# Hybrid decoder layer with 64 experts: the shared expert's down products in nine pieces, the first token lists among its gate and up tiles, the sorting in seven steps

## What is computed

```python
def _moe(x, p):
    scores = sigmoid(xf @ p['w_router'])              # 264 x 64
    ...                                               # group-limited top 8 of 64 experts
    gate = sum(one_hot(eidx, 64) * wsel[..., None])   # weight of each token for each expert
    def expert_block(xb, gb):
        h = silu(einsum('td,edf->tef', xb, w_gate)) * einsum('td,edf->tef', xb, w_up)
        h = h * gb[..., None]
        return einsum('tef,efd->td', h, w_down)       # w_gate, w_up: 1024x256, w_down: 256x1024 each
    routed = expert_block(...)
    shared = (silu(xf @ p['ws_gate']) * (xf @ p['ws_up'])) @ p['ws_down']
    return routed + shared

y = h + _moe(rmsnorm(h)); output = rmsnorm(y)
```

## Time and profile before

| what | us |
|---|---|
| median of 3 runs | 1104.72 |
| the three runs | 1104.01, 1104.72, 1107.85 |
| span of the profiled execution, first to last instruction | 1106.8 |
| TensorE busy | 967.0 (87%) |
| VectorE busy | 531.6 (48%) |
| GpSimd busy | 347.4 (31%) |
| ScalarE busy | 230.3 (21%) |

### The profile page before, as it was taken

The page is one execution under the profiler, slowest core; times in us unless marked ns, Lnnn a source line. Parts: engine busy times, 40 slices in busy tenths (PEclk is TensorE's granted clock), DMA queues, the critical chain, the costliest instruction groups (busy, mean ns, idle before and its releaser), DMA issues. The chain is left out here.

```text
span 1106.8 us, 17738 instructions
## 1 busy us (share of the span) xinstructions
PE 967.0 (87%) x7221; PEld 564.4 (51%) x7221; DVE 531.6 (48%) x1014; ACT 230.3 (21%) x476; POOL 347.4 (31%) x396
## 2 busy tenths in 40 slices
PE   5999999999999978788998798897987878789896
PEld 4878777877877775356333333333333323323231
DVE  2158759766875868745621111111112335424685
ACT  3241134115113411430211111111111111111012
POOL 0059609914970892001011101101013213312330
PEclk9999999999999998889999998988989888989999
DMA  8535244234524192395699999999999999999931
GB/s 236 188 118 183 97 131 168 108 125 131 189 85 154 45 330 73 155 359 187 239 394 418 418 417 412 412 404 405 401 403 400 401 375 379 401 415 402 387 98 41
DMA packets 98972, 295.65 MB, mean 267 GB/s; under 512 B 19603, under 2 KB 50901, under 8 KB 82232
## 3 DMA queue, kind: packets, MB, share of 16 engines
q1 hardware_dynamic: 80695, 254.02, 60.1%
q0 software_dynamic: 18192, 40.46, 9.8%
HBM read 284.12 MB, written 36.30 MB: 290 GB/s over the span
## 5 line engine op out<-in xcount | busy, mean ns | idle before, releaser
L1278 PE MATMUL bank<-big 64*64 64x64 f32 (+7 forms) x6778 | 910.9, 367 | 117.1 <-DMA big<-in_w_up 70.5
L1278 PEld LDWEIGHTS bank<-big 64*64 64x64 f32 (+3 forms) x6778 | 516.7, 152 | 462.1 <-issue 378.6
L1577 ACT ACTIVATE big<-bank 128x512 f32<-128x512 f32 (+6 forms) x283 | 121.2, 450 | 714.6 <-PE bank L1278 396.9
L1075 POOL DMA_INDIRECT big<-xg,big x32 | 32.3, 1008 | 404.2 <-PE bank L561 353.3
L919 DVE TENSOR_TENSOR big<-big,bank 128x256 f32<-128x256 f32 x32 | 13.4, 420 | 239.3 <-ACT big L1577 239.3
L2069 POOL TENSOR_SCALAR big<-big 128x256 f32<-128x256 f32 x120 | 124.5, 1038 | 1.7
L2081 POOL TENSOR_TENSOR big<-big 128x256 f32<-128x256 f32 x120 | 86.2, 718 | 0.3
L1867 DVE SCALAR_TENSOR_TENSOR big<-big 128x256 f32<-128x256 f32 x120 | 78.7, 656 | 4.1
L979 DVE SCALAR_TENSOR_TENSOR big<-big 128x1024 f32<-128x1024 f32 (+1 forms) x48 | 61.4, 1280 | 17.3 <-DMA big<-yrows,big 14.1
L1092 POOL DMA_INDIRECT big<-yrows,big x48 | 51.2, 1067 | 51.0 <-DVE big L979 28.4
L1577 ACT ACTIVATE big<-big 128x272 f32<-128x272 f32 (+8 forms) x104 | 48.2, 509 | 46.7 <-DVE big L814 12.3
(11 more groups left out here) (163 smaller groups left out, 406.5 us busy)
## 6 DMA issues: line engine op xcount, KB each, us to landing
big<-in_w_gate SPq DMA_DIRECT2D x64, 1024.0 KB, 15.8
big<-in_w_up SPq DMA_DIRECT2D x64, 1024.0 KB, 20.4
big<-in_w_down SPq DMA_DIRECT2D x64, 1024.0 KB
big<-in_w_in SPq DMA_DIRECT2D x29, 1024.0 KB, 5.3
yrows<-big POOLq DMA_DIRECT2D x32, 512.0 KB, 3.5
big<-in_w_out SPq DMA_DIRECT2D x2, 2048.0 KB, 16.2
big<-in_state_wkv SPq DMA_DIRECT2D x32, 64.0 KB, 2.2
out_wkv_s<-big SPq DMA_DIRECT2D x32, 64.0 KB, 3.8
```

The lines of the kernel that those rows point to most:

```text
L1075: pool.indirect_dma_start(out=x[0:n, :], out_offset=None, in_=xg, in_offset=bass.IndirectOffsetOnAxis(ap=idxu[0:n, col:col + 1], axis=0), ...
L1278: return nc.tensor.matmul(out_, lhsT=lhsT, rhs=rhs, start=start, stop=stop)
L1577: return nc.scalar.activation(out_, in_, f, **kw)
```

## The change

- The shared down matrix is no longer loaded first into slot 3; it is loaded after the gate and up of expert 3 into a place of its own, `wsd` (two of the five row buffers `early` that are first used in pair 19). SP no longer waits for `shd_mm`; the down matrix of expert 3 is loaded with the first loads.
- The down products are cut into nine pieces: four of 256 columns for each block of 128 rows (two matmuls each), and one for the sample rows (eight matmuls). TensorE does piece n at the start of iteration 4 + n, between `index` and the first half of `gate_up`. All use one half of bank 5, whose other half takes the turned hidden values; so `turn_hidden(q-1)` in that iteration also waits until the piece has been added (`shy_ready`).
- VectorE adds piece n in `pair(4 + n)`, ahead of `hidden`; for the sample rows ScalarE copies and VectorE adds in pair 12.
- The tiles `shared_gate_up(1, 0)` and `(1, 1)` are cut into halves, and the lists 0, 1 and 2 and `turn(0)` stand between the halves.
- The sorting becomes a generator, `rows_and_gates`, of which one step is done after each of `pair(1)` to `pair(7)`. The two buffers that hold `wsd` are no longer cleared; the third is cleared by VectorE in the last step and not by GpSimd ahead of pair 0.

A load that waited for the down products is replaced by one that waits for nothing of its own. The diff, cut:

```diff
@@ moe_sp
-            for part, n in enumerate(('ws_gate', 'ws_up', 'ws_down')):
+            for part, n in enumerate(('ws_gate', 'ws_up')):
                 load_item(sp, part, SHARED_SLOT, A[n][0])
...
+            load_item(sp, 2, 3, expert_w(2, 3))
...
-            sp.wait_ge(S['shd_mm'], 5)
-            load_item(sp, 2, 3, expert_w(2, 3))
+            sp.dma_start(wsd, A['ws_down'][0].rearrange("(j p) d -> p j d", p=128)).then_inc(S['wsd_in'], 16)
@@ moe_pe
+            def shared_down(n):
+                if n == 0:
+                    pe.wait_ge(S['wsd_in'], 16)
+                    pe.wait_ge(S['shh_ready'], 2)
+                wait(pe, 'shy_ready', n)
+                t, i = divmod(n, 4)
                 for j in range(2):
...
+                    if t < 2:
+                        ins = mm(ps_sd, hsh[:, j, 128 * t:128 * t + 128], wsd[:, j, QD * i:QD * i + QD], j == 0, j == 1)
+                    else:
+                        for i in range(4):
+                            ins = mm(ps_sd[32 * i:32 * i + NS, :], hsh[:, j, NP:NT], wsd[:, j, QD * i:QD * i + QD],
+                                     j == 0, j == 1)
                 note(ins, 'shd_mm')
...
@@ turn_hidden
+                if 0 < q + 2 - DOWN_AT < NDOWN:
+                    pe.wait_ge(S['shy_ready'], q + 2 - DOWN_AT)
+                elif q + 2 - DOWN_AT == NDOWN:
+                    pe.wait_ge(S['shs_ready'], 6)
...
-            for q in range(3):
-                index(q)
-            shared_gate_up(1, 1)
-            pe.wait_ge(S['shh_ready'], 2)
-            pe.wait_ge(S[f'wd_in{SHARED_SLOT}'], 16)
-            shared_down(0)
+            index(0)
+            shared_gate_up(1, 0, KT // 2, KT)
+            index(1)
+            shared_gate_up(1, 1, 0, KT // 2)
+            index(2)
             pe.wait_ge(S['cnt_ready'], 1)
             turn(0)
+            shared_gate_up(1, 1, KT // 2, KT)
...
-                if q == 0:
-                    pe.wait_ge(S['shy_ready'], 2)
+                if q == 1:
+                    pe.wait_ge(S['shh_ready'], 2)
+                if DOWN_AT <= q < DOWN_AT + NDOWN:
+                    shared_down(q - DOWN_AT)
                 gate_up(q, 0, 4)
-                if q == 0:
-                    shared_down(1)
-                    shared_down(2)
...
@@ moe_dve
+                if DOWN_AT <= q < DOWN_AT + NDOWN - 1:
+                    shared_rows(q - DOWN_AT)
                 hidden(q)
...
+            rows = rows_and_gates()
             for q in range(1, NPAIR):
                 pair(q)
+                next(rows, None)
@@ moe_pool
-            for x in early[2:]:
-                link(gp.memset(x, 0.0), 'xe_zero')
...
```

More of the change, by code:

```diff
@@ L755, in moe_act @@
             turned(0)
-            act.wait_ge(S['shd_mm'], 5)
-            for i in range(4):
-                note(fn(shs[0:NS, QD * i:QD * i + QD], ps_sd[4][32 * i:32 * i + NS, 0:QD], ACT.Copy), 'shs_ready')
             for q in range(NPAIR):
+                if q == DOWN_AT + NDOWN - 1:
+                    act.wait_ge(S['shd_mm'], NDOWN)
+                    for i in range(4):
+                        note(fn(shs[0:NS, QD * i:QD * i + QD], ps_sd[32 * i:32 * i + NS, :], ACT.Copy), 'shs_ready')
                 if q:
@@ L904, in shared_hidden, with shared_rows @@
                 note(v.tensor_tensor(hsh[:, j, :], sgs[:, j, :], ps_sh[2 + j][:, 0:NT], M), 'shh_ready')
-            def shared_rows(t):
-                for h in range(2):
-                    dve.wait_ge(S['shd_mm'], 2 * t + h + 1)
-                    x = xrow[:, t, 512 * h:512 * h + 512]
-                    note(v.tensor_tensor(x, x, ps_sd[2 * t + h][:, :], AD), 'shy_ready')
+            def shared_rows(n):
+                t, i = divmod(n, 4)
+                if t < 2:
+                    dve.wait_ge(S['shd_mm'], n + 1)
+                    x = xrow[:, t, QD * i:QD * i + QD]
+                    note(v.tensor_tensor(x, x, ps_sd, AD), 'shy_ready')
+                else:
+                    dve.wait_ge(S['shs_ready'], 6)
+                    note(v.tensor_tensor(xrow[0:NS, 2, :], xrow[0:NS, 2, :], shs[0:NS, :], AD), 'shy_ready')
             onehot(0)
```

113 lines of the change are left out of this document (59 added, 54 removed).

## The result

The changed kernel takes 1094.38 us (median of 4 runs, 1092.86 to 1096.27) beside 1105.84 us for the kernel before on the same chip (1104.01 to 1107.85): a ratio of 0.9892, with a 95% interval of 0.9869 to 0.9915. That is 11.5 us less. Two later comparisons of the same two kernels gave 0.9923 (0.9899 to 0.9947) and 0.9895 (0.9868 to 0.9922), so the gain is some 8.5 to 12 us. The profiled execution of the changed kernel took 1092.86 us around a span of 1091.1 us. In every run here 1.8 us lie around the span, so the profiled execution of the kernel before, with its span of 1106.8 us, took about 1108.6 us: it is none of the four, and some 2.8 us above their median. Its trace stands for a somewhat long execution.

The account below looks back on a forecast made before the run. The prediction took the weight stream to bound the expert loop, its unbroken start setting the end. 12.0 us up to pair 0 plus 0.5 from the sorting made 12.5, from 1104.72 to 1092.2 us, range 1088.5 to 1098.

Parts of the forecast that it names:

- The end follows the start of the stream, not TensorE's work: Expert loop: weights set the pace, so bringing SP's releases at 538.35 and 551.16 us forward brings all that follows forward.
- 12.0 us up to the end of pair 0: Token mask to pair 0's gate and up: 12.2 us removed, 0.2 us waiting at `turn(0)`, ending 12.0 us earlier at 526.2.
- parts for the down products: Before and inside pair 0: moving the shared down products away takes off 4.1 us and 4.8 us.
- part for the lists: Shared tiles before pair 0: two 0.66 us waits for list row numbers go, 1.3 us, and the slow clock behind, 2.0.
- counter-entry: At `turn(0)`, now earlier: gather 0 lands at 515.5 us against TensorE's arrival at 515.4, a wait of 0.2 us.
- signs I had named for being wrong: TensorE waiting over 1 us at `turn(0)`, pairs 4 to 12 over 17 us, or the lead shrinking from pair 4 to 27.
- first rival: At `turn(0)`: gather 0 lands 3.0 us late, slow clock follows; gain only 7.8 to 9.5 us, 1095.2 to 1096.9; chance 0.14.
- 0.5 us from the sorting: Pair 2: the 2.56 us `onehot` wait and slow clock go, 4.3 us on TensorE; 0.5 us stays, between 0 and 1.5.
- Pieces at cost 0: Pairs 4 to 12: 8.5 us of pieces run inside waits for weights of 2.6 us per pair, costing 0.
- slower rival: Pairs 4 to 12: TensorE waits in `turn_hidden` for VectorE's adding, 5.2 us more per pair; 1115.6 us; chance 0.05.
- marks I had named: Signs of being right: timeline moments from pair 0 to pair 27, no L882 wait at pair 2, none at `turn_hidden`.
- dry stream of pair 22: Pair 22 lost 3.1 us at 203 GB/s; one such place more gives 1095.3, one less 1089.1; beyond that band chance 0.07.

Follow-up runs that it names:

- pieces alone: The changed kernel with lists and sorting put back as before, so only the nine down-product pieces and SP's order differ from the kernel before: 1096.42 us, ratio 0.9917.
- pieces three times: The changed kernel with the matmuls of each of the nine pieces done three times over, 17 us more on TensorE: 1096.15 us, ratio 0.9923.

## Why the prediction was right

The forecast was 1092.2 us with a range of 1088.5 to 1098.0, and 12.5 us of gain; the time is 1094.4 and the gain 11.5 (8.5 to 12 over three comparisons). Between forecast and result the median of the kernel before has moved from 1104.72 us (three runs) to 1105.84 (four), which is 1.1 of the 2.2 us between 1092.2 and 1094.4; the gain is 1.0 us under the forecast in this comparison, and 0.5 to 4 us over all three. The direction, the mechanism and the place held. One term was too large, by 3.1 us, and that the first comparison came within 1 us all the same is in part luck.

- **The end follows the start of the stream, not TensorE's work.** Held: the table above, and 17 us of added work for 0 to 3 us of time. What I called the unbroken stream begins, by the holes in it, at the *down* release of pair 0, not behind expert 3. In the queue's terms: between the gate-up and the down release SP may issue four matrices (10 us at 417 GB/s), the releases are 12.8 us apart, so the queue runs dry there, with `ws_down` in it or not. From the down release on a release brings six matrices (15 us), and the next two come 12.8 and 13.2 us apart, so a queue builds up.
- **12.0 us up to the end of pair 0.** Here the size was off: 8.9. The parts for the down products (4.1 and 4.8) are right to 0.3 us: the kernel with the pieces alone has its release 9.2 us earlier. The part for the lists (1.3 and 2.0) was right as far as it went, and its counter-entry was not: **I took gather 0 near its free time, 0.2 us of waiting, and it was 1.8 to 2.1 us**, and the slow clock behind a wait, which I had charged to the old kernel's waits and not to this new one, took 1.6 to 1.9 us more. That was one of the signs I had named for being wrong, a wait of over 1 us at `turn(0)`, and it came true: this part of the prediction was wrong, though the time wasn't. On the clock of the kernel before it landed at 517.2 (515.41, and 1.82 us for the mask that came that much sooner), not at 515.5. The Trainium skill (DMA: Bandwidth & Descriptors, Queues, rings and completion order) has each DMA engine take its queues in turn, a packet from each, and I had worked out 515.5 from even turns and 516 to 517 from one queue for all: the measured landing, the 1.7 to 1.9 us that one MB more added, and the bytes that came only behind the weights' are on the side of the single queue. The page's rule, read as even turns by bytes, isn't borne out here; how large the packets of either side were, no run here shows. This was the first rival, with a landing 3.0 us late and the slow clock behind it; it had 0.14 of the chances. In mechanism it is what happened, and its 7.8 to 9.5 us of gain are the size at the start (8.9, and 0.5 more would be from the sorting). The time of the first comparison still fell into the forecast's band of 1089.1 to 1095.2. The forecast's place and this rival's were 3 us apart, within the measurement's reach only over several comparisons.
- **0.5 us from the sorting (0 to 1.5).** Where the pieces are moved, the traces give 1.7 us at pair 12 (206.0 against 204.3); alone it gives 0. The reason is the one named (the queue runs low before the next release), with a length I hadn't worked out: 6 MB last 15 us, and the second release came 19.2 us behind the first with the sorting in a block.
- **Pieces at cost 0.** Held: in pairs 4 to 12 the waits for weights fell from 23 to 18 us in 8 places, and no wait at `turn_hidden` appears. With a piece in each, pairs 4 to 12 follow each other by 17.0 us, as pairs 12 to 16 do. The waits I had put at 1.7 us each came out at 1.9 on average in pairs 5 to 12, but unevenly (below). The slower rival's mechanism isn't in any trace.
- **The marks I had named.** Gate and up of pair 0 near 526: 527.6. Down release near 539: 540.5. Pair 4 near 572 with a wait of 4 us: 572.2 with 2.9. Pair 27 near 975: 973.9. They agree better than they should, since the whole profiled execution was 1.8 us ahead at the mask already: counted from the mask they are 3.2, 3.2, 2.0 and 0.7 us late. Whether the distance to before shrinks between pair 4 and pair 27, another sign I had named, isn't clear: it goes from 10.8 to 11.4 us in the first execution of the changed kernel, from 10.3 to 10.0 and from 10.2 to 10.4 in the other two.
- **The dry stream of pair 22**: in one execution of the changed kernel it was gone, in two it was there. So it differs between executions of one program, and the rival was right to leave both directions open; what decides it no run here shows.
- **A slip in the reading of the slices**. The stretch that begins at 553 us and moves 375 to 418 GB/s starts with the twenty-first slice; the twentieth has 239. Nothing in the sum hangs on it.

## What to carry to other kernels

In a loop paced by loads, look for the first release from which the queue never empties again, and take work off the way to *that* moment, even if it costs as much in a place where the engine waits for loads anyway. Moving a load into an idle stretch ahead of it gains nothing if the queue empties once more before that release. And where an edit brings a consumer forward, ask what its producer's transfer will meet: a small gather beside queued weights took 5.8 us instead of 3.5, and one more half tile of work ahead of the wait brought the release 3.3 to 3.6 us forward.

The lowest time of these kernels is that of the changed one with `turn(0)` behind the last half tile: 1092.18 us, 0.9881 of before. The intervals don't set it apart from the later down load of expert 4 (0.9885). The two in one kernel weren't tried.

## What the runs showed that I had not expected

- A wait of 1.8 us for gather 0 was followed by 0.57 of the granted clock over 4 us, a wait of 0.66 us twice by 0.68 (before), and the work behind either took 1.6 to 2 us longer. The waits and what follows them cost about the same. But a wait of 1.54 us at the same place was followed by none (pieces three times), and neither was one of 2.02 us at pair 4 of the kernel before, whose first half took 3.65 us.
- One MB of weights more in the queues made the gather 1.7 to 1.9 us later, near the 2.5 us that 1 MB takes at 417 GB/s: the gather had little of the engines for itself.
- The waits for weights in the changed kernel (first execution) alternate from pair 5 on: 3.2 to 4.5 us in one pair and 0.3 to 1.3 (once none) in the next, where before they were some 2.5 us each. The period is the same, 17 us. Behind the long waits a first half takes 6.3 to 6.6 us, behind the short ones 3.65, so a pair that waited long ends late and leaves less of a wait to the next.
